# Residual rows moved to DRAM for the expert blocks, a fourth pair of weight buffers, and a transposition moved into block 14

## The chip, the core and the metric

The kernel runs on one core of a Trainium2 chip. The core has TensorE (PE), VectorE (DVE), ScalarE (ACT), GpSimd (POOL), SyncE (SP) and 16 DMA engines. The engines run their own instruction streams and wait for one another through semaphores. The metric is the time of one execution on the device, in microseconds.

## What is computed

A layer on 512 tokens of width 1024: RMSNorm, a mixer (state-space heads beside gated recurrent heads) with a residual addition, then a second RMSNorm and a mixture of 16 experts in four groups. Each token takes its best group and two experts in it. All of it is in float32.

```python
# in the layer
x = x + jnp.concatenate([y_ssd, y_hgrn], axis=-1) @ w_out[l]
h = rmsnorm(x, norm_ffn_w[l])
x = x + hier_moe(h, router_group[l], router_expert[l], w_gate[l], w_up[l], w_down[l])
...
# in hier_moe, for each expert
hid = jax.nn.silu(t @ wg) * (t @ wu)
return acc + c[:, None].astype(t.dtype) * (hid @ wd), None
...
return rmsnorm(x, final_norm_w)
```

## The kernel before

**Stages.** The front (to about 296 us) computes the mixer, the residual rows `xres` (512 rows of 1024 floats, 2 MB of SBUF in `arena`), and the normalised rows, which ScalarE stores to `h2_dram` in four column units (`store_rows`, L890). Routing follows: which tokens go to which expert. Then 16 expert blocks run, and at the end the two results of each token are read back, weighted, added to the residual row and normalised.

**A block** handles one expert `e`: GpSimd gathers up to 112 token rows from `h2_dram` into one of four buffers (`gather`, L645); TensorE transposes them; ScalarE and DVE make a high and a low part of everything that is multiplied (float32 as the sum of two reduced numbers, three products each). The weights are three loads of 1 MB: `a` (first half of gate and up, K rows 0 to 511), `b` (second half) and `c` (down). High parts come from ScalarE (`round_a`, `round_b`, `round_c`), the low part of `a` from GpSimd (`split_a`), those of `b` and `c` from DVE (`split_b` L1444, `split_c` L1450). TensorE does `gate_up_a`, `gate_up_b`; ScalarE the silu, DVE the product `hid` (`hidden`, L1456). TensorE transposes `hid` into bank 4, ScalarE rounds it to `hidh` (L969), DVE subtracts to `hidl` (L1467), and TensorE makes the down product in two halves of 512 columns (banks 5 and 6). ScalarE copies these out and GpSimd scatters them to `pairs_dram` (L675).

**Order.** `pe_expert(e)` is written out by hand and runs one block ahead: `gate_up_a(e+1)`, transposition of hid(e), transposition of the tokens of e+2, `gate_up_b(e+1)`, down product of e. In the last two blocks some of these drop out.

**Loads.** SP issues the weight loads in one fixed order, `a`(e), `c`(e-1), `b`(e). There are three buffers of each kind (`WSETS`). Before each load SP waits until the buffer's last user is split: `wla_ok`, `wlb_ok`, `wlc_ok`. SP issues in order, so a load whose buffer is free still waits behind an earlier one that waits. `b`(3) also waits for the first gather (`gat_in[0]`). After the last weights SP loads the early half of the result rows (`load_early`, L526), which DVE adds to `xres` (L1510, `early`), then, after the last scatter, the late half (`late`).

## Time and profile before

| | us |
|---|---|
| three runs: median (lowest to highest) | 490.27 (490.12 to 491.42) |
| the profiled execution: its time | 490.27 |
| its span, first to last instruction | 488.5 |
| TensorE busy | 445.9 (91% of the span) |
| DVE, ScalarE, GpSimd busy | 340.3, 272.2, 147.9 |
| DMA | 92.47 MB, 189 GB/s over the span |

Matmuls are pipelined, so TensorE's busy time is not its time at full rate. The mean granted clock of TensorE is 0.968 of full speed. The profiled execution's own time is that of the median, so differences worked out on its span can be added to the median. A wait shown for an engine is put down to the releaser that came last.

### The profile page before, as it was taken

The page shows a single profiled execution, that of the slowest core. Times are in us where ns is not written, and L with a number is a line of the kernel's source. Part 1 is how long each engine was busy: PE and PEld are TensorE (multiplying, and loading weights), DVE is VectorE, ACT ScalarE, POOL GpSimd, SP SyncE. Part 2 cuts the span into 40 slices and gives each one's busy share as a digit, 9 for nine tenths or more (in the row PEclk, how much of TensorE's full clock was granted, in tenths as well). Part 3 has the DMA queues.
Part 4 walks back from the last instruction along what each step waited for, and adds up shares of the span by engine and source line. Part 5 has one row for each costly group of instructions (what it writes and reads, how often), then busy time and mean ns, then how long its engine had stood idle before and what let it go on. Part 6 is the DMA issues. An engine that isn't in the chain of part 4 may idle for free.

```text
span 488.5 us, 7225 instructions
## 1 busy us (share of the span) xinstructions
PE 445.9 (91%) x2827; PEld 393.7 (81%) x2827; DVE 340.3 (70%) x517; ACT 272.2 (56%) x440; POOL 147.9 (30%) x113
## 2 busy tenths in 40 slices
PE   5999999999999899999899997799999999999800
PEld 3888888899898799999899996688888888887600
DVE  5424798754669777799856428678788788767847
ACT  6754273423553243226344326489899899979524
POOL 4700000000000000110510120567887987875210
PEclk9999999999999989999899998999999999999965
DMA  8622222231202111206086931569999999988345
GB/s 320 236 95 87 87 88 86 87 129 44 87 1 86 60 34 82 86 8 253 0 336 243 335 129 44 161 253 378 363 382 372 358 367 380 357 331 318 128 154 225
DMA packets 20626, 92.47 MB, mean 189 GB/s; under 512 B 4797, under 2 KB 7017, under 8 KB 12138
## 3 DMA queue, kind: packets, MB, share of 16 engines
q1 hardware_dynamic: 13848, 81.42, 44.3%
q0 software_dynamic: 4096, 8.41, 5.1%
q10 hardware_dynamic: 2642, 2.11, 1.4%
q8 instruction: 24, 0.39, 0.3%
q14 instruction: 16, 0.13, 0.1%
HBM read 86.69 MB, written 11.54 MB: 201 GB/s over the span
## 4 chain that ended last, share of the span: by engine, by line
PE 69%; DVE 13%; DMA 8%; ACT 7%; issue 2%; POOLq 0%; SPq 0%; DVEq 0%; ACTq 0%
PE bank L1578 40%; DMA arena<-in_w_gate_up_dram 5%; PE bank L1896 4%; PE bank L1898 4%; PE bank L1897 4%; PE bank L1884 2%; PE bank L1750 1%; PE bank L1766 1%; DMA pairs_dram<-arena 1%; DVE wl L1031 1%; DMA X<-h_dram,arena 1%; ACT wh L907 1%; PE bank L1648 1%; DVE arena L1542 1%; PE bank L1649 1%
## 5 line engine op out<-in xcount | busy, mean ns | idle before, releaser
L1578 PE MATMUL bank<-wh,acth 128*128 128x256 f32 x320 | 93.2, 291 | 3.3 <-DVE actl L1025 1.9
L1578 PE MATMUL bank<-wl,acth 128*128 128x256 f32 x320 | 91.8, 287 | 0.0
L1578 PE MATMUL bank<-wh,actl 128*128 128x256 f32 x320 | 91.7, 287 | 0.0
L1578 PEld LDWEIGHTS bank<-wh,acth 128*128 128x128 f32 x320 | 62.8, 196 | 3.7 <-issue 3.7
L665 POOL TENSOR_TENSOR wl<-raw,wh 128x1024 fp32r<-128x1024 f32 x21 | 50.6, 2432 | 47.3 <-ACT wh L902 47.3
L611 POOL TENSOR_TENSOR arena<-arena,bc 128x512 f32<-128x512 f32 x4 | 6.6, 1655 | 190.6 <-DVE arena L1106 190.6
L1578 PEld LDWEIGHTS bank<-wl,acth 128*128 128x128 f32 x320 | 62.9, 196 | 0.0
L1578 PEld LDWEIGHTS bank<-wh,actl 128*128 128x128 f32 x320 | 62.7, 196 | 0.0
L1896 PE MATMUL bank<-wh,acth 128*128 128x512 f32 x128 | 51.7, 404 | 1.4 <-DVE wl L1447 1.2
L1898 PE MATMUL bank<-wh,actl 128*128 128x512 f32 x128 | 50.1, 392 | 0.0
L1897 PE MATMUL bank<-wl,acth 128*128 128x512 f32 x128 | 49.9, 390 | 0.0
L1578 PE MATMUL bank<-acth,wh 128*128 128x512 f32 x112 | 44.1, 393 | 0.0
L1578 PE MATMUL bank<-acth,wl 128*128 128x512 f32 x112 | 43.6, 390 | 0.0
L1578 PE MATMUL bank<-actl,wh 128*128 128x512 f32 x112 | 43.6, 389 | 0.0
L721 ACT ACTIVATE wh<-raw 128x2048 fp32r<-128x2048 f32 x18 | 34.4, 1910 | 15.4 <-PE bank L1578 15.4
L1031 DVE TENSOR_TENSOR wl<-raw,wh 128x2048 fp32r<-128x2048 f32 x15 | 34.3, 2288 | 3.5 <-ACT wh L721 3.4
L1453 DVE TENSOR_TENSOR actl<-arena,acth 128x1024 fp32r<-128x1024 f32 x30 | 35.7, 1229 | 1.4 <-ACT acth L916 1.0
L1441 DVE TENSOR_TENSOR actl<-bank,acth 128x512 fp32r<-128x512 f32 x32 | 20.6, 686 | 18.2 <-ACT acth L954 18.0
L1447 DVE TENSOR_TENSOR wl<-arena,wh 128x1024 fp32r<-128x1024 f32 x20 | 27.0, 1388 | 8.2 <-ACT wh L907 8.2
L916 ACT ACTIVATE acth<-arena 128x1024 fp32r<-128x1024 f32 x30 | 30.0, 1056 | 0.0
L1896 PEld LDWEIGHTS bank<-wh,acth 128*128 128x128 f32 x128 | 24.0, 188 | 7.2 <-issue 2.1
L654 POOL DMA_INDIRECT X<-h_dram,arena x16 | 26.5, 1659 | 8.0 <-issue 6.8
(335 smaller groups left out, 1039.1 us busy)
## 6 DMA issues: line engine op xcount, KB each, us to landing
raw<-in_w_units_dram SPq DMA_DIRECT2D x18, 1024.0 KB, 4.8
raw<-in_w_gate_up_dram SPq DMA_DIRECT2D x17, 1024.0 KB, 11.1
arena<-in_w_down_dram SPq DMA_DIRECT2D x16, 1024.0 KB
arena<-in_w_gate_up_dram SPq DMA_DIRECT2D x15, 1024.0 KB, 12.5
arena<-pairs_dram SPq DMA_DIRECT2D x6, 512.0 KB, 6.5
X<-in_x_dram SPq DMA_DIRECT2D x4, 512.0 KB, 5.1
arena<-in_x_dram SPq DMA_DIRECT2D x1, 2048.0 KB, 9.9
h_dram<-X ACTq DMA_DIRECT2D x4, 512.0 KB, 4.0
```

The source lines that it names most:

```text
L654: gp.indirect_dma_start(hg[j][0:CAP, :], None, h2_dram, bass.IndirectOffsetOnAxis(ap=gix[0:CAP, PERM[e]:PERM[e] + 1], axis=0), bounds_chec ...
L665: gp.tensor_tensor(wl[:, 0, c], raw_a[b][:, c], wh[:, 0, c].bitcast(F32), ALU.subtract).then_inc(wla_ok, 1)
L721: sc.activation(wh[:, u % SPL, :], raw[:, u % RAW, :], ACT.Copy).then_inc(wh_ok, 1)
L916: sc.activation(down_high(e)[:, c], raw_c[e % WSETS][:, c], ACT.Copy).then_inc(whc_ok, 1)
L1031: ve.tensor_tensor(wl[:, u % SPL, :], raw[:, u % RAW, :], wh[:, u % SPL, :].bitcast(F32), ALU.subtract).then_inc(wl_ok, 1)
L1441: ve.tensor_tensor(gtl[b][:, c], bank[2 + h][:, :], gth[b][:, c].bitcast(F32), ALU.subtract).then_inc(gl_ok, 1)
L1447: ve.tensor_tensor(wl[:, 1, c], raw_b[e % WSETS][:, c], wh[:, 1, c].bitcast(F32), ALU.subtract).then_inc(wlb_ok, 1)
L1453: ve.tensor_tensor(down_low(e)[:, c], raw_c[e % WSETS][:, c], down_high(e)[:, c].bitcast(F32), ALU.subtract).then_inc(wlc_ok, 1)
L1578: ins = te.matmul(acc_ap, a, b, start=(j == 0), stop=(j == n - 1))
L1896: te.matmul(bank[b][:, :], ah, uh[:, k, :], start=(first and k == 0), stop=False)
L1897: te.matmul(bank[b][:, :], ah, ul[:, k, :], start=False, stop=False)
L1898: ins = te.matmul(bank[b][:, :], al_, uh[:, k, :], start=False, stop=(last and k == kh - 1))
```

## The change

The residual rows are stored to a new DRAM tensor `res_dram`, unit by unit, right behind each store of the normalised rows on ScalarE's DMA queue. The 2 MB of SBUF that they leave become a fourth buffer for `a` and one for `b` (`AB = 4`); `c` keeps three. SP loads `a`(3) and `b`(3) into them once all four residual stores have landed (`res_st`). The wait for the first gather is gone. After the last weights SP reads the residual rows back into `raw` (slots 0 and 2, `back`), before it reads the early result rows; these have one semaphore now in place of four. In block 14 TensorE transposes hid(15) between the two halves of its down product, and ScalarE and DVE write its two parts to `turn2` instead of `hidh`, `hidl`, which block 14 still reads.

```diff
@@ -261,7 +262,10 @@
         rnd = part(4)
         rounds = part(1).bitcast(I32)
 
+        raw_a += [arena[:, TT * D:TT * D + UNIT]]
+        raw_b += [arena[:, TT * D + UNIT:TT * D + 2 * UNIT]]
         early = [raw[:, 1, 0:D], raw[:, 1, D:2 * D], arena[:, 0:D], arena[:, D:2 * D]]
+        back = [raw[:, j, :].rearrange("p (t n) -> p t n", t=2) for j in (0, 2)]
         late = [arena[:, a:a + D] for a in range(8 * D, 12 * D, D)]
         assert ofs[0] <= 22528
 
@@ -271,6 +275,12 @@
 
         def down_low(e):
             return wl[:, 0, :] if e == NE - 1 else wcl
+
+        def hidden_high(e):
+            return turn2[:, 0, :] if e == NE - 1 else hidh[:, :]
+
+        def hidden_low(e):
+            return turn2[:, 1, :] if e == NE - 1 else hidl[:, :]
 
         gth = [acth[:, UNIT + b * D:UNIT + (b + 1) * D] for b in range(2)]
         gtl = [actl[:, UNIT + b * D:UNIT + (b + 1) * D] for b in range(2)]
@@ -493,48 +505,53 @@
...
             def sp_round(r, base, first_round=False):
-                for e in range(WSETS if first_round else 0, NE + 1):
-                    held = base + e - WSETS + 1 if e >= WSETS else base
+                for e in range(AB if first_round else 0, NE + 1):
+                    held = base + e - AB + 1 if e >= AB else base
                     if e < NE:
-                        if e == WSETS + 1:
+                        if e == AB + 1:
                             sp.wait_ge(gu_a, base + 2)
+                        elif e == 0:
+                            sp.wait_ge(early_ok, r * TT)
                         else:
-                            wait_a(sp, r, max(e - WSETS + 1, 0))
+                            wait_a(sp, r, max(e - AB + 1, 0))
                         load_a(e)
-                    if e - 1 >= (WSETS if first_round else 0):
+                    if e >= 1:
                         before_c = base + e - WSETS if e > WSETS else base
                         sp.wait_ge(wlc_ok, before_c * 2)
                         load_c(e - 1)
                     if e < NE:
-                        if e == 0:
-                            sp.wait_ge(early_ok, r * TT)
-                        else:
-                            sp.wait_ge(wlb_ok, held * 2)
-                        if first_round and e == WSETS:
-                            sp.wait_ge(gat_in[0], 16)
+                        sp.wait_ge(wlb_ok, held * 2)
                         load_b(e)
 
-            def load_early(rows_done, first_round=False):
+            def load_back(rows_done, first_round=False):
+                if first_round:
+                    wait_a(sp, 0, NE - 3)
+                    sp.wait_ge(wlb_ok, (NE - 3) * 2)
+                else:
+                    sp.wait_ge(sca_out[0], rows_done)
+                for j in range(2):
+                    sp.dma_start(back[j], res_dram[2 * j * P:2 * (j + 1) * P, :].rearrange("(t p) n -> p t n", p=P))\
+                        .then_inc(xres_in, 16)
                 for j in range(YB):
                     sp.wait_ge(sca_out[j], rows_done)
                 if first_round:
                     wait_a(sp, 0, NE - 2)
                     sp.wait_ge(wlb_ok, (NE - 2) * 2)
                 for tt in range(TT):
-                    sp.dma_start(early[tt], pairs_dram[tt * P:(tt + 1) * P, :]).then_inc(early_in[tt], 16)
+                    sp.dma_start(early[tt], pairs_dram[tt * P:(tt + 1) * P, :]).then_inc(early_in, 16)
 
             def sp_later(r, base):
                 sp_round(r, base)
-                load_early(r * (16 * PER_Y) + 16 * PER_Y)
+                load_back(r * (16 * PER_Y) + 16 * PER_Y)
 
             load_c(0)
             split_by(sp, n_in + 1)
@@ -548,10 +565,13 @@
             load_b(0)
             load_b(2)
             load_c(2)
+            sp.wait_ge(res_st, 16 * (n_front - n_in))
+            load_a(3)
+            load_b(3)
             sp_round(0, 0, True)
             sp.wait_ge(h2_ok, 2 * (n_front - n_in))
             sp.dma_start(bc[:, :], final_norm_w[None, :].broadcast_to([P, D])).then_inc(bc3_in, 16)
-            load_early((PER_Y - 1) * 16, True)
+            load_back((PER_Y - 1) * 16, True)
             n = later_rounds(sp, sp_later)
             for j in range(YB):
                 sp.wait_ge(sca_out[j], n * (16 * PER_Y))
@@ -891,27 +911,28 @@
                 act.wait_ge(h2_ok, unit_end[u] - n_in_groups)
                 c = slice(units[u][1], units[u][1] + UC)
                 act.dma_start(h2_dram[:, c].rearrange("(t p) n -> p t n", p=P), X[:, :, c]).then_inc(h2_st, 16)
+                act.dma_start(res_dram[:, c].rearrange("(t p) n -> p t n", p=P), xres[:, :, c]).then_inc(res_st, 16)
...
@@ -958,6 +979,10 @@
                 sc.activation(sil, bank[e % 2][:, 0:FE], ACT.Silu,
                               scale=hg[e % HGB][:, D:D + 1]).then_inc(sil_ok, 1)
 
+            def round_hidden(step, e):
+                act.wait_ge(hid_tr, step + 1)
+                sc.activation(hidden_high(e), bank[4][:, 0:FE], ACT.Copy).then_inc(hh_ok, 1)
+
             def act_expert(r, base, e, first_round):
                 step, b = base + e, e % 2
                 if 0 < e < NE - 1:
@@ -965,8 +990,8 @@
                 if e + 2 < NE:
                     act.wait_ge(gu_a, step + 2)
                     round_a(r, e + 2, (0,))
-                act.wait_ge(hid_tr, step + 1)
-                sc.activation(hidh[:, :], bank[4][:, 0:FE], ACT.Copy).then_inc(hh_ok, 1)
+                if e < NE - 1:
+                    round_hidden(step, e)
                 if e + 2 < NE:
                     round_a(r, e + 2, (1,))
                     round_tokens(step + 2, b)
@@ -976,6 +1001,8 @@
                     silu(step + 1, e + 1)
                 if e + 2 < NE:
                     round_b(r, e + 2)
+                elif e + 1 < NE:
+                    round_hidden(step + 1, e + 1)
                 act.wait_ge(dn, step * 2 + 3)
                 y_free(act, r, e, first_round)
                 sc.activation(ysb[e % YB][:, 0:512], bank[5][:, :], ACT.Copy).then_inc(y0_ok, 1)
@@ -1505,10 +1533,11 @@
                     dve_expert(r, base, e, first_round)
                 if first_round:
                     gates()
+                dve.wait_ge(xres_in, r * 32 + 48)
+                dve.wait_ge(early_in, r * (16 * TT) + 16 * TT)
                 for tt in range(TT):
-                    dve.wait_ge(early_in[tt], r * 16 + 16)
-                    ve.scalar_tensor_tensor(early[tt], early[tt], r1[:, 10, tt:tt + 1], xres[:, tt, :], ALU.mult,
-                                            ALU.add).then_inc(early_ok, 1)
+                    ve.scalar_tensor_tensor(early[tt], early[tt], r1[:, 10, tt:tt + 1], back[tt // 2][:, tt % 2, :],
+                                            ALU.mult, ALU.add).then_inc(early_ok, 1)
 
             def gates():
                 dve.wait_ge(ge_ok, 1)
@@ -1914,15 +1943,19 @@
                 pe.wait_ge(wlb_ok, step * 2 + 2)
                 gate_up(b, 1, range(4), False, True).then_inc(gu_b, 1)
 
-            def pe_expert(r, base, e):
-                step, b = base + e, e % 2
-                if e + 1 < NE:
-                    gate_up_a(r, step + 1, e + 1, 1 - b)
+            def turn_hidden(step):
                 pe.wait_ge(hid_ok, step + 2)
                 pe.wait_ge(hl_ok, step + 1)
                 for k in range(2):
                     ins = te.transpose(bank[4][:, k * P:(k + 1) * P], hid[:, k * P:(k + 1) * P], ident[:, :])
                 ins.then_inc(hid_tr, 1)
+
+            def pe_expert(r, base, e):
+                step, b = base + e, e % 2
+                if e + 1 < NE:
+                    gate_up_a(r, step + 1, e + 1, 1 - b)
+                if e < NE - 1:
+                    turn_hidden(step)
                 if e + 2 < NE:
                     turn_tokens(r, base, e + 2)
                 if e + 1 < NE:
@@ -1936,8 +1969,11 @@
                     terms = []
                     for k in range(2):
                         c, n = slice(k * P, (k + 1) * P), slice(h * 512, (h + 1) * 512)
-                        terms += [(hidh[:, c], c3h[:, k, n]), (hidh[:, c], c3l[:, k, n]), (hidl[:, c], c3h[:, k, n])]
+                        hh, hl = hidden_high(e)[:, c], hidden_low(e)[:, c]
+                        terms += [(hh, c3h[:, k, n]), (hh, c3l[:, k, n]), (hl, c3h[:, k, n])]
                     products(bank[5 + h][:, :], terms).then_inc(dn, 1)
+                    if e == NE - 2 and h == 0:
+                        turn_hidden(step + 1)
 
             def pe_round(r, base):
                 find_all(r)
```

The rest of the diff: `set_uses` gets the number of buffers, and `% WSETS` becomes `% AB` for the `a` and `b` buffers in the splits.

SP's queue around the first expert blocks. `raw` and `arena` hold the buffers; `in_w_gate_up_dram` is `a` (L496) or `b` (L499), `in_w_down_dram` is `c`. Before, from `a`(3) to `b`(4):

```order
L496 DMA raw<-in_w_gate_up_dram 128x2048 [waits wla_ok]
L499 DMA raw<-in_w_gate_up_dram 128x2048 [waits gat_in0,wlb_ok]
L496 DMA raw<-in_w_gate_up_dram 128x2048 [waits gu_a]
L502 DMA arena<-in_w_down_dram 128x2048 [waits wlc_ok]
L499 DMA arena<-in_w_gate_up_dram 128x2048 [waits wlb_ok]
```

After (L508 is `a`, L511 is `b`, L514 is `c`), from `a`(3) to `a`(5):

```order
L508 DMA arena<-in_w_gate_up_dram 128x2048 [waits res_st]
L511 DMA arena<-in_w_gate_up_dram 128x2048
L508 DMA raw<-in_w_gate_up_dram 128x2048 [waits wla_ok]
L514 DMA arena<-in_w_down_dram 128x2048 [waits wlc_ok]
L511 DMA raw<-in_w_gate_up_dram 128x2048 [waits wlb_ok]
L508 DMA raw<-in_w_gate_up_dram 128x2048 [waits gu_a]
```

`a`(3) and `b`(3) wait for the residual stores only, no load waits for the gather any more, and the wait for `gu_a` stands at `a`(5), behind `c`(3) and `b`(4), where it stood ahead of them at `a`(4).

TensorE's queue at the end of the blocks: the down product of block 14 (`acth`, `actl` hold its weights, `hidh`, `hidl` the products), the transposes (`ident`) and the down product of block 15 (weights in `wh`, `wl`). Before:

```order
L1578 MATMUL bank<-actl,hidh 128x512
L1578 MATMUL bank<-acth,hidl 128x512
L1924 MATMUL bank<-ident,arena 128x128 [waits hl_ok,hid_ok]
L1924 MATMUL bank<-ident,arena 128x128
L1578 MATMUL bank<-wh,hidh 128x512 [waits y0_ok,wlc_ok,hl_ok]
```

After, where the same two transposes stand:

```order
L1607 MATMUL bank<-actl,hidh 128x512
L1607 MATMUL bank<-acth,hidl 128x512
L1950 MATMUL bank<-ident,arena 128x128 [waits hl_ok,hid_ok]
L1950 MATMUL bank<-ident,arena 128x128
L1607 MATMUL bank<-acth,hidh 128x512 [waits y1_ok]
```

They moved from behind the second half (which waits for `y1_ok`) to ahead of it; the down product of block 15 now follows the second half directly and reads `turn2`.

## Rows read from the trace of the kernel before

**Rows 1.** The page's slices of 12.2 us: DMA engines' busy tenths.
```profile
DMA  8622222231202111206086931569999999988345
```

**Rows 2.** Waits of PE, 230 to 489: in total, times, longest us.
```profile
PE bank L1884 <- DMA X<-h_dram,arena: 2.5, 1, 2.5
...
PE bank L1855 <- DVE arena L1385: 2.0, 1, 2.0
...
PE bank L1578 <- DVE hidl L1467: 1.2, 1, 1.2
...
PE bank L1896 <- DVE wl L1447: 1.2, 2, 0.8
```

**Rows 3.** The chain that ended last: start us, us, what.
```profile
304.90 4.35 DMA X<-h_dram,arena
...
416.17 24.49 DMA arena<-in_w_gate_up_dram
...
465.65 5.16 DMA pairs_dram<-arena
```

**Rows 4.** PE in order of time: start us, us, line, form, [idle before].
```profile
430.22 0.39 PE L1896 MATMUL bank<-wh,acth 128*128 128x512 f32 x1
...
439.56 0.39 PE L1896 MATMUL bank<-wh,acth 128*128 128x512 f32 x1
...
450.26 0.39 PE L1896 MATMUL bank<-wh,acth 128*128 128x512 f32 x1
...
453.99 0.47 PE L1896 MATMUL bank<-wh,acth 128*128 128x512 f32 x1 [0.43 <-DVE wl L1447]
...
461.13 0.50 PE L1578 MATMUL bank<-wh,hidh 128*128 128x512 f32 x1 [1.20 <-DVE hidl L1467]
```

**Rows 5.** ACT in order of time, the second half `b` of expert 14.
```profile
440.68 2.01 ACT L907 ACTIVATE wh<-arena 128x1024 fp32r<-128x1024 f32 x2 [3.10 <-DMA arena<-in_w_gate_up_dram]
```

**Rows 6.** DMA issues of windows 295.5, 329, 338, 404, 322, 406.7, 444: KB, us to landing.
```profile
h_dram<-X ACTq DMA_DIRECT2D x1, 512.0 KB, 3.4
...
pairs_dram<-arena POOLq DMA_INDIRECT x1, 6.9
...
pairs_dram<-arena POOLq DMA_INDIRECT x1, 9.6
...
pairs_dram<-arena POOLq DMA_INDIRECT x1, 12.2
...
arena<-in_w_gate_up_dram SPq DMA_DIRECT2D x1, 1024.0 KB, 9.1
...
arena<-in_w_gate_up_dram SPq DMA_DIRECT2D x1, 1024.0 KB, 22.4
...
arena<-pairs_dram SPq DMA_DIRECT2D x2, 512.0 KB, 13.2
```

**Rows 7.** SP's queue in order of time: start us, us, what is issued.
```profile
284.48 0.33 SPq L496 DMA_DIRECT2D raw<-in_w_gate_up_dram  x1
...
309.33 0.33 SPq L499 DMA_DIRECT2D raw<-in_w_gate_up_dram  x1
...
321.17 0.33 SPq L496 DMA_DIRECT2D raw<-in_w_gate_up_dram  x1
...
332.18 0.46 SPq L499 DMA_DIRECT2D arena<-in_w_gate_up_dram  x1
...
336.49 0.33 SPq L496 DMA_DIRECT2D raw<-in_w_gate_up_dram  x1
```

**Rows 8.** Busy us of each engine, granted clock, DMA share, GB/s in a stretch.
```profile
300.00:304.00 4.00, 3.99 (x38) 3.93 (x39) 3.00 (x14) 2.03 (x3) 0.00 (x0) 0.58 0.00 0
```

**Rows 9.** DVE in order of time, from block 14 to the end.
```profile
456.38 2.35 DVE L1453 TENSOR_TENSOR wl<-arena,wh 128x1024 fp32r<-128x1024 f32 x2
458.64 0.47 DVE L1458 SCALAR_TENSOR_TENSOR arena<-bank,X,arena 128x256 f32<-128x256 f32 x1
...
474.29 2.58 DVE L1536 SCALAR_TENSOR_TENSOR arena<-arena,raw 128x1024 f32<-128x1024 f32 x2 [6.61 <-DMA arena<-pairs_dram]
```

More of the change, by code:

```diff
@@ L135, in trunk @@
     WSETS = 3
+    AB = 4
     HGB = 4
@@ L404, in trunk @@
         fin_ok = sem("fin_ok")
-        ra_in, rb_in, rc_in = ([sem(f"{n}{b}") for b in range(WSETS)] for n in ("ra_in", "rb_in", "rc_in"))
+        ra_in, rb_in = ([sem(f"{n}{b}") for b in range(AB)] for n in ("ra_in", "rb_in"))
+        rc_in = [sem(f"rc_in{b}") for b in range(WSETS)]
         gat_in = [sem(f"gat_in{j}") for j in range(HGB)]
         sca_out = [sem(f"sca_out{j}") for j in range(YB)]
-        early_in = [sem(f"early_in{t}") for t in range(TT)]
+        early_in = sem("early_in")
+        res_st = sem("res_st")
         late_in = [sem(f"late_in{t}") for t in range(TT)]
@@ L421, in trunk @@
         PERM = [(e % G) * EG + e // G for e in range(NE)]
-        IN_SET = [(NE - w + WSETS - 1) // WSETS for w in range(WSETS)]
         PER_Y = NE // YB
@@ L432, in later_rounds, with set_uses @@
             return n
-        def set_uses(r, e):
-            return r * IN_SET[e % WSETS] + e // WSETS + 1
+        def set_uses(r, e, sets):
+            return r * ((NE - e % sets + sets - 1) // sets) + e // sets + 1
         def y_free(eng, r, e, first_round):
@@ L495, in load_a @@
             def load_a(e):
-                sp.dma_start(raw_a[e % WSETS], w_gate_up[PERM[e], 0]).then_inc(ra_in[e % WSETS], 16)
+                sp.dma_start(raw_a[e % AB], w_gate_up[PERM[e], 0]).then_inc(ra_in[e % AB], 16)
             def load_b(e):
-                sp.dma_start(raw_b[e % WSETS], w_gate_up[PERM[e], 1]).then_inc(rb_in[e % WSETS], 16)
+                sp.dma_start(raw_b[e % AB], w_gate_up[PERM[e], 1]).then_inc(rb_in[e % AB], 16)
             def load_c(e):
@@ L658, in split_a @@
             def split_a(step, e):
-                b = e % WSETS
+                b = e % AB
                 for h in range(2):
@@ L899, in round_a @@
             def round_a(r, e, which=(0, 1)):
-                act.wait_ge(ra_in[e % WSETS], set_uses(r, e) * 16)
+                act.wait_ge(ra_in[e % AB], set_uses(r, e, AB) * 16)
                 for c in halves(which):
-                    sc.activation(wh[:, 0, c], raw_a[e % WSETS][:, c], ACT.Copy).then_inc(wha_ok, 1)
+                    sc.activation(wh[:, 0, c], raw_a[e % AB][:, c], ACT.Copy).then_inc(wha_ok, 1)
             def round_b(r, e):
-                act.wait_ge(rb_in[e % WSETS], set_uses(r, e) * 16)
+                act.wait_ge(rb_in[e % AB], set_uses(r, e, AB) * 16)
                 for c in halves((0, 1)):
-                    sc.activation(wh[:, 1, c], raw_b[e % WSETS][:, c], ACT.Copy).then_inc(whb_ok, 1)
+                    sc.activation(wh[:, 1, c], raw_b[e % AB][:, c], ACT.Copy).then_inc(whb_ok, 1)
             def round_c(r, base, e):
@@ L1466, in dve_expert @@
                 dve.wait_ge(hh_ok, step + 1)
-                ve.tensor_tensor(hidl[:, :], bank[4][:, 0:FE], hidh[:, :].bitcast(F32), ALU.subtract).then_inc(hl_ok, 1)
+                ve.tensor_tensor(hidden_low(e), bank[4][:, 0:FE], hidden_high(e).bitcast(F32),
+                                 ALU.subtract).then_inc(hl_ok, 1)
                 if e + 2 < NE:
```

5 lines of the change are left out of this document (3 added, 2 removed).

## The prediction

> **What bounds the kernel now.** I read first the row of the DMA engines' busy tenths over the 40 slices (12.2 us each) [rows 1]: 3, 1 and 5 tenths in slices 24 to 26 (281 to 317 us), then 6, eight times 9 and twice 8 (317 to 452 us), which is where the expert blocks run. Next, who waited for whom, on TensorE from 230 us on [rows 2]: in the blocks it waits in three places only: 2.5 us for the first gathered tokens, 1.2 us for the low part of weights (DVE L1447, the subtraction for a second half `b`), and 1.2 us for `hidl` in the last block. The chain that ended last [rows 3] runs through the same places: the gather of expert 0 (304.90, 4.35 us), then a `b` load that took 24.49 us, then the last scatter. TensorE sets the pace between 311 and 464 us, fed by a DMA that can only just keep up, and the start of the blocks hangs on one gather.
>
> The blocks themselves, from the first matmul of `gate_up_a` [rows 4]: 430.22 to 439.56 is 9.34 us for a block without a stall, 439.56 to 450.26 is 10.70 us. Block 15's `gate_up_b` should start 2.94 us after its `gate_up_a` (12 matmuls at 0.227 us and two transposes), so at 453.20; it starts at 453.99. The late weights thus cost 1.36 + 0.79 = 2.15, say **2.2 us**. Why they are late: ScalarE waits 3.10 us for `b` of expert 14 [rows 5]. The time from issue to landing of a `b` load grows from 9.1 us (expert 4, issued at 322.0) to 22.4 us (expert 13, issued at 406.8) [rows 6]: 13.3 us over nine blocks, 1.5 us per block. The DMA needs about 10.8 us for what a block of 9.33 us uses, and lives on its lead.
>
> **The fourth pair and the order of the loads.** Where the loads are issued now [rows 7]: `a`(3) at 284.48, `b`(3) at 309.33 (held until the first gather has landed), `a`(4) at 321.17 with `c`(3) and `b`(4) behind it, `c`(4) and `b`(5) at 332, `a`(6) at 336.49. After the change `a`(3), `b`(3) wait for the residual stores. The last h2 store takes 3.4 us from issue [rows 6]; the residual store of equal size goes behind it and adds 0.524 MB at some 340 GB/s, 1.5 us: issued at 296.0, landed at about 301. `a`(3), `b`(3) and `a`(4) then go out in a row at 301 to 302 and `c`(3), `b`(4) at about 310.5, when DVE has split `c`(0). `a`(5) waits for `gu_a`, 321.2. From there SP's order decides: `c`(4) still needs the three-deep `c` buffers (the split of `c`(1), 331.8), and `b`(5) stands behind it in SP's queue, so `b`(5) goes out at 332.2 **as before**, and only `a`(6) is early, by 4 us, in a queue that is full anyway. The fourth pair does not give a block's lead; it gives a queue that is emptier at 332 us.
> How much emptier: before, six loads were issued from 321.2 to 332.2. By row `b`(4), three loads and the latency take 9.9 us (321.17 to 331.1), and later loads 3.6 us each (10.8 by three), so `b`(5) lands at some 341.5. After, `c`(4) and `b`(5) meet an empty queue: two loads, 7.2 us less what the emptiness saves, landing at 338 to 340. The lead gained is 1.5 to 3.6 us, I take 2.6. `b`(14) was 3.1 us late at ScalarE and becomes 0.5 late; 1.06 us of lateness one block earlier cost TensorE nothing, the block of `a`(15) starting on its 9.34 us. Both late subtractions are then in time: **−2.2 us** (bounds −1.0, if the lead is 1.5 and the gain half, and −2.2, since no more is lost there). What is next: TensorE itself at 9.33 us per block.
>
> **The price at the start.** Between 300 and 304 us the DMA share is 0.00 today, and the gather of expert 0 has the engines to itself: 4.35 us from 304.90 [rows 3, 8]. After, it enters at about 306.2, behind three weight loads of 1 MB (8.5 us of transfers from 303 on). No row shows a gather under load with its landing. The nearest are scatters of equal size on the same queue [rows 6]: 6.9 us (329, three or four loads outstanding), 9.6 us (338), 12.2 us (404, a deep backlog), against 5.16 us alone (465.65) [rows 3]. So load costs +1.7, +4.4 or +7.0 us. At 306 three loads are outstanding, as at 329 and 338: between +1.7 and +4.4, **+3.3 us** taken. Lower bound 0.5 (the gather is a read and reaches few rows), upper +7, which would also take in expert 1's gather: it is issued 1.5 us after the first and is needed 4.9 us after it. All of it is on the path: TensorE, ScalarE (high part) and DVE (low part) wait for this landing in turn.
> The trace shows full DMA share with the scatter still through in 6.9 us, far less than the backlog of the weight queue. The Trainium skill (DMA: Bandwidth & Descriptors, Queues, rings and completion order) says that each DMA engine takes turns between its queues, a packet at a time. By that rule a gather shares instead of queueing, about doubling its moving part of 2 to 3 us: the sum would be nearer +2 than +3.3, and both stay inside the bounds.
>
> **The residual rows.** Added: four stores of 0.5 MB on ScalarE's queue, two reads of 1 MB, four times 0.4 us of ScalarE for issuing. The first three stores fall before 281 us, where the loads in flight are wanted no sooner than 296; ScalarE has 0.8 us of idle time after each. The store of `rs` moves behind the last residual store, from 299.3 to about 301; the gather itself waits for the index table until 303.5. Cost 0, cover 2.5 us; past it each us counts. SP waits at `res_st` instead of loading `a`(3) at 284.48: wanted at 330, cost 0. At the end the reads (5.6 us of DMA time) stand between `c`(15) and the early rows, which landed 13.2 us after issue at 444.43 [rows 6], at 457.6: with the reads at about 463, less the lead. DVE's additions of the early rows end 6.61 us before 474.29, at 467.7, and then it waits for the late rows [rows 9]; they take 5 us, so they begin at 462.8. Cost 0 while the reads delay them by less than 6.6 us, beyond that fully. DVE, waiting there, has nothing else queued but the final sums.
>
> **Block 14.** Today the last transposes follow the down product of block 14; ScalarE and DVE then make hidh and hidl, and the down product of block 15 starts at 461.13 after a wait of 1.20 us [rows 4], 1.36 us after the transposes end. Now the transposes go between its two halves of 1.38 us. But hid(15) must exist: DVE L1458 ends at 459.11, behind the split of `c`(15) (456.38, 2.35 us) [rows 9], whereas the first half ends at 458.18. On this trace TensorE would wait 1.0 us in the middle and gain only 0.35. With `b`(15) in time the same order gives more: `gate_up_a` of block 15 starts at D, the first half ends at D+7.1, hid is ready at D+7.5 by these durations, the second half ends at D+9.2, and block 15's down product starts there instead of at D+10.0. **−0.8 us** (bounds −0.3 and −1.4, the whole wait).
>
> **Sum** against the profiled execution (span 488.5, time 490.27, which is also the median): +3.3 − 2.2 − 0.8 = +0.3, so a span of 488.8 and **490.6 us**. The tail after the last matmul, 24 us, stays.
>
> **Rivals.**
> (1) The gather is hardly disturbed (up to +1.5). Then 490.27 + 1.0 − 3.0 = **488.3**, faster. For: only three loads are outstanding and the shallowest scatter lost 1.7. Against: 9.6 us at 338 with the same number.
> (2) The start slips by 5 us or more: gather 0 at +4.4 to +7 and gather 1 behind it in the same queue late as well, or TensorE's clock falls. It was granted 0.58 from 300 to 304 [rows 8], the lower level of 1.2 GHz for most of it, after a wait of 2.0 us for the routing [rows 2]; after the 2.5 us at 306.8 it stayed high. With the idle time at 5 us or more a second fall may follow, costing some 1.7 us of doubled matmuls. 490.27 + 5.5 − 3.0 = **492.8**, up to 495. It decides once the gather takes more than 8.7 us.
> (3) The lead does nothing at the end: the queue fills again at 1.5 us per block and `b`(14), `b`(15) are as late, since SP's order issues them when it did. Then +3.3 − 0.3 (block 14 on late weights) gives **493.3**. Against: a later start of TensorE gives the DMA that much more time before each need, so part of the lateness goes in any case.
> (4) The change doesn't do what it says: `b`(e) is not issued earlier from expert 5 on. That is already in the sum.
>
> **How the numbers follow.** Forecast case (+1.5 to +4.5 at the start, stalls gone): 0.45, own range 488.9 to 491.8. Rival 1: 0.27. Rival 2: 0.18. Rival 3: 0.10. The range 487.3 to 494.3 leaves out the ends of rivals 1 and 2. A measurement can tell 0.3% (1.5 us) from no change: faster means under 488.8, slower over 491.7. Rival 1 nearly all faster, with a little of the forecast case: 0.30. Rivals 2 and 3 and the upper end of the forecast case: 0.32. Same: 0.38.
>
> **What would show it.** Gather of expert 0 from issue to landing 7 to 8 us instead of 4.35, TensorE's first wait 5 to 6 us instead of 2.5. `a`(3) issued at 301, `b`(5) within 0.5 us of `c`(4). No wait of ScalarE for a `b` load above 2 us and no TensorE wait for DVE L1447's successor. A short TensorE wait between the halves of block 14, none before block 15's down product. DVE's early additions no later than 468 relative to the same end. Wrong if the gather lands in 5 us, if `b` loads late in the run still take over 22 us, or if the late rows are waited for longer than 6.6 us.

## The result and the profile after

| | before | after |
|---|---|---|
| median of one job, us | 489.21 (20 runs) | 492.6 (20 runs) |
| span of the profiled execution | 488.5 | 492.1 |
| DMA | 92.47 MB, 189 GB/s | 96.67 MB, 196 GB/s |

The ratio is 1.0071, 95% interval 1.0049 to 1.0092: the change costs 3.5 us (2.4 to 4.5). I had said 490.6 on 490.27 for the likeliest case, inside 0.3% of no change; the time lies in the range of the prediction, but above that case. By the 0.3% that I had set as the border it is slower, to which I had given 0.32 (no change 0.38).

The page's slices of 12.3 us of the kernel after, the DMA engines' busy tenths; they answer to [rows 1]:

```profile
DMA  8622223240202213033189908727999999989455
```

Slices 25 and 26 (295 to 320 us), which hold the gather, have 8 and 7 tenths where there were 1 and 5; slices 27 and 28 have 2 and 7 where [rows 1] has 6 and 9. The loads moved forward, and behind them a hole opened.

TensorE's waits after, from 230 us on (in total, times, longest), as in [rows 2]; L1925 is the second half of gate and up, L1950 the transposition of `hid`:

```profile
PE bank L1913 <- DMA X<-h_dram,arena: 5.8, 1, 5.8
PE bank L1884 <- DVE arena L1412: 2.0, 1, 2.0
...
PE bank L1925 <- DVE wl L1474: 1.0, 2, 0.6
PE bank L1950 <- DVE arena L1485: 0.8, 1, 0.8
```

The wait for the gathered tokens grew from 2.5 to 5.8 us; that for the low part of `b` is still there; the 1.2 us for `hidl` became 0.8 us between the halves of block 14. The chain that ended last (start us, us, what) runs through the same three transfers as in [rows 3]:

```profile
302.86 7.79 DMA X<-h_dram,arena
...
419.65 24.70 DMA arena<-in_w_gate_up_dram
...
469.02 5.35 DMA pairs_dram<-arena
```

The gather takes 7.79 us instead of 4.35, the `b`(14) load 24.70 instead of 24.49, the last scatter 5.35 instead of 5.16.

TensorE in order of time, after:

```profile
310.69 1.97 PE L1913 MATMUL bank<-ident,X 128*128 128x128 f32 x8 [5.84 <-DMA X<-h_dram,arena]
312.45 1.91 PE L1589 MATMUL bank<-upto,ones 128*128 128x128 f32 x8
314.01 0.77 PE L1925 MATMUL bank<-wh,acth 128*128 128x512 f32 x1
...
462.89 0.44 PE L1950 MATMUL bank<-ident,arena 128*128 128x128 f32 x2 [0.80 <-DVE arena L1485]
463.08 0.48 PE L1607 MATMUL bank<-acth,hidh 128*128 128x512 f32 x1
...
464.56 0.40 PE L1607 MATMUL bank<-wh,turn 128*128 128x512 f32 x1
```

The eight transposes after the gather take 1.97 us; at the end of a gather that came in 4.2 us (version e1, below) the same eight take 1.09. So TensorE comes back at half its clock. The windows say the same (stretch; its length; busy time of PE, its weight loads, DVE, ScalarE and GpSimd, each with a count; granted clock; DMA share; GB/s):

```profile
305.00:307.00 2.00, 0.00 (x0) 0.00 (x0) 2.00 (x3) 0.00 (x0) 1.70 (x2) 1.00 1.02 426
307.00:309.00 2.00, 0.00 (x0) 0.00 (x0) 1.49 (x2) 0.00 (x0) 1.70 (x2) 1.00 0.77 239
309.00:311.00 2.00, 0.31 (x2) 0.32 (x3) 0.00 (x0) 0.00 (x0) 0.50 (x1) 0.53 0.81 257
311.00:313.00 2.00, 2.00 (x11) 2.00 (x10) 0.53 (x1) 0.91 (x2) 0.00 (x0) 0.50 1.03 287
313.00:315.00 2.00, 2.00 (x9) 1.82 (x8) 0.85 (x2) 0.29 (x1) 0.00 (x0) 0.50 1.01 353
```

TensorE idles from 304.85 to 310.69; the clock falls from 2.4 to 1.2 GHz at about 309, before the tokens are there, and stays there until after 315.

**Where the 3.6 us of span come from.** Each execution can be cut at the same four points of TensorE's queue. G is the time from the issue of the first gather to the first transposes of its tokens, C from there to the transposes of expert 1's tokens, then come twelve blocks, and E is the time from the transposes of expert 13's tokens to the last matmul. The twelve blocks take 109.56 to 109.60 us in all fourteen profiles of this study; so all that differs is in G, C, E, in the front (to the gather's issue) and in the tail (last matmul to the end).

| | front | G | C | E | tail |
|---|---|---|---|---|---|
| before | 304.90 | 4.39 | 4.95 | 40.34 | 24.33 |
| after | 302.86 | 7.83 | 7.05 | 40.21 | 24.57 |
| difference | −2.04 | +3.44 | +2.10 | −0.13 | +0.24 |

The sum is +3.6 us. The front's −2.04 can't be put down to the change: the front ends between 301.6 and 304.9 in the fourteen executions, at 303.2 on average in the four without the residual stores and at 303.7 in the ten with them. The tails lie between 23.7 and 25.8. The gather gives +3.44, the lower clock +2.10, and the end, where I had taken off 3.0 us, gives back 0.1.

### The profile page after: what moved, and what is told of

Its sections match the earlier page's. It is cut to its first block, busy times and chain, and to the rows that moved or that the text cites. A ratio compares the mean times of both kernels' runs of the same rounds, so it can differ in the third digit from the quotient of the medians.

```text
span 492.1 us, 7231 instructions
## 1 busy us (share of the span) xinstructions
PE 446.3 (91%) x2827; PEld 393.5 (80%) x2827; DVE 340.3 (69%) x517; ACT 272.3 (55%) x440; POOL 147.2 (30%) x113
## 2 busy tenths in 40 slices
DMA packets 23282, 96.67 MB, mean 196 GB/s; under 512 B 4893, under 2 KB 9161, under 8 KB 14794
## 4 chain that ended last, share of the span: by engine, by line
PE 68%; DVE 14%; DMA 9%; ACT 7%; issue 2%; POOLq 0%; SPq 0%; DVEq 0%; ACTq 0%
PE bank L1607 39%; DMA arena<-in_w_gate_up_dram 5%; PE bank L1925 4%; PE bank L1927 4%; PE bank L1926 4%; PE bank L1913 2%; DMA X<-h_dram,arena 2%; DMA pairs_dram<-arena 1%; PE bank L1779 1%; PE bank L1795 1%; DVE actl L1480 1%; DVE wl L1058 1%; ACT wh L928 1%; PE bank L1589 1%; PE bank L1677 1%
## 5 line engine op out<-in xcount | busy, mean ns | idle before, releaser
L1925 PE MATMUL bank<-wh,acth 128*128 128x512 f32 x128 | 52.3, 409 | 1.1 <-DVE wl L1474 1.0
L685 POOL TENSOR_TENSOR wl<-raw,wh 128x1024 fp32r<-128x1024 f32 x15 | 36.0, 2419 | 50.1 <-ACT wh L923 50.1
L685 POOL TENSOR_TENSOR wl<-arena,wh 128x1024 fp32r<-128x1024 f32 x16 | 39.0, 2457 | 13.0 <-ACT wh L923 13.0
L1474 DVE TENSOR_TENSOR wl<-arena,wh 128x1024 fp32r<-128x1024 f32 x24 | 33.6, 1438 | 9.0 <-ACT wh L928 8.9
L1925 PEld LDWEIGHTS bank<-wh,acth 128*128 128x128 f32 x128 | 24.3, 190 | 7.1 <-issue 1.9
```

Of the source, the lines that this page charges most:

```text
L685: gp.tensor_tensor(wl[:, 0, c], raw_a[b][:, c], wh[:, 0, c].bitcast(F32), ALU.subtract).then_inc(wla_ok, 1)
L1474: ve.tensor_tensor(wl[:, 1, c], raw_b[e % AB][:, c], wh[:, 1, c].bitcast(F32), ALU.subtract).then_inc(wlb_ok, 1)
L1925: te.matmul(bank[b][:, :], ah, uh[:, k, :], start=(first and k == 0), stop=False)
```

## Experiments

Ratios are to the kernel before in the same job, with their 95% interval. All profiles are cut at the points named above. In a clean end, with no weight late, E is 37.01 us with the move in block 14 (e2, f2, g1) and 38.12 without it (g2); "late" is E less that.

**e1: the gather alone again.** The kernel after, with `a`(3) and `b`(3) held until the first gather has landed:

```diff
             sp.wait_ge(res_st, 16 * (n_front - n_in))
+            sp.wait_ge(gat_in[0], 16)
             load_a(3)
             load_b(3)
```

> The changed kernel, but SP also waits for the first gather before it loads a(3), b(3), a(4). My theory: the disturbed gather (7.79 us in place of 4.35) and the slow matmuls behind it (2.1 us) are the whole loss. Then the gather lands in 4.3 to 4.6 us, transposes of expert 1 follow the first gather by 5.0 us in place of 7.05, and the time falls 5 us below the changed kernel, to 1 to 2 us below the kernel before if the block 14 edit gives 0.3 and the late weights stay as they are. Rival: the loss is the extra 4 MB of traffic or the later a(3); then the time stays within 1 us of the changed kernel (3.4 us over before).

Measured: ratio 1.0006 (0.9979 to 1.0032). G 4.20, C 4.94, E 39.18, so late 2.17. The loss is gone, so it sat at the start. No gain is left over, though there are four pairs of halves.

What the gather meets: DMA packets of the kernel after in the first 4 us from the gather's issue (q1 is SP's queue, q0 the one of the gather):

```profile
DMA packets 224, 1.70 MB, mean 426 GB/s; under 512 B 16, under 2 KB 16, under 8 KB 16
## 3 DMA queue, kind: packets, MB, share of 16 engines
q1 hardware_dynamic: 223, 1.70, 100.6%
```

and in the rest, up to its landing at 310.65:

```profile
q0 software_dynamic: 337, 0.58, 52.5%
q1 hardware_dynamic: 58, 0.34, 23.9%
```

In e1, in the same first 4 us and, in the second fence, without the first 1.5 of them (304.67 to 308.67, and 306.17 to 308.67):

```profile
q0 software_dynamic: 176, 0.25, 26.6%
```

```profile
q0 software_dynamic: 176, 0.25, 42.5%
```

The count is the same, so none moves in the first 1.5 us; in e1 and in the kernel before the first packet comes 1.8 to 1.9 us after the issue. Under three weight loads not one of them moves in the first 4 us, while q1 fills all 16 engines; its first packet comes 4.4 to 4.5 us after the issue, as the loads run out. The five executions with these three loads ahead of the gather (after, e3, f2, f3, f4) show what the start follows: counted from the gather's own issue the first packet comes after 3.5 to 4.5 us, counted from the issue of `a`(3) after 8.8 to 9.1 us in all five. So the gather does not share with the loads, it begins behind them, and then takes some 3.3 us (7.79 less 4.45) for what takes 2.5 alone (4.35 less 1.85). The Trainium skill (DMA: Bandwidth & Descriptors, Queues, rings and completion order) says that an engine goes round the queues that have work, packet by packet; what the trace shows between 304.4 and 306.9 is no such turn-taking, and both queues are at work only after that. Whether this goes against the page stays open: if the gather's descriptors came late, its queue had no work to take turns with; if they were there, its packets were passed over. No run here tells the two apart.

**e3 and f3: is it the clock?** The kernel after, with more dummy matmuls while TensorE waits for the gather; nothing reads their result. e3 has 36 more, f3 has 24 more:

```diff
                 find_targets(r)
-                keep_warm(4)
+                keep_warm(4 + 36)
                 turn_tokens(r, base, 0)
```

> The changed kernel with 36 more dummy matmuls of 128 columns ahead of the first token transposes, so that TensorE is busy for 5 of the 5.8 us in which it waits for the gather. Theory: the slow transposes and the slow first matmuls (0.63 to 0.77 us each) come from the longer idle time. Then the transposes take 1.1 us as before, the expert 1 transposes follow by 5.0 us in place of 7.05, and the time is 2 us below the changed kernel. Rival: the slow start is something else, such as reads of tokens under DMA load; then nothing changes, within 0.5 us.

> As e3_warm with 24 repetitions in place of 36: there the dummies ran on for about 2 us after the gather had landed, and with them the matmuls behind ran at full clock. Theory: with 24 they end within 0.5 us of the landing, the slow matmuls stay away, and the time from the gather's issue to the end of the last down product is 162.3 to 163 us in place of 164.7 of the changed kernel; 1.5 to 2.3 us under the changed kernel by the clock. Rival: within 0.5 us of the changed kernel.

Measured: e3 1.0100 (1.0066 to 1.0134), f3 1.0041 (1.0019 to 1.0063); the kernel after, again beside f3 in one job, 1.0088 (1.0053 to 1.0123). In e3 the dummies run until 314.2, past the landing: G is 9.92 and C 4.87. They cost 2.1 us of G and give 2.2 of C, and the time is no better than that of the kernel after. In f3 they end as the tokens come, TensorE in order of time:

```profile
305.64 6.50 PE L1589 MATMUL bank<-upto,ones 128*128 128x128 f32 x56
312.29 0.98 PE L1913 MATMUL bank<-ident,X 128*128 128x128 f32 x7 [0.15 <-DMA X<-h_dram,arena]
```

G is 7.58, as in the kernel after, and C is 4.93 in place of 7.05. Full clock, same gather: f3 is 2.3 us faster than the kernel after by the ratios, where the two C differ by 2.1. The intervals overlap, so the time alone would not prove it; profile and time together say that the clock costs about 2 us.

**f4: the change again**, as it is.

> The changed kernel again, beside the others on the same chip. Theory: 3.4 us over before (1 to 5.5), the gather lands 7.5 to 8 us after its issue and slow matmuls follow it. Rival: the clock fell only in the one profiled execution; then the gather is as slow here but the tokens of expert 1 are turned 4.9 to 5.1 us after those of expert 0.

Its profile has G 7.75 and C 7.09, as in the first one. But E is 38.08: late 1.07 instead of 3.20. The late weights differ by 2 us between two executions of one kernel, so one profile can't price them; this bears on every E here.

**e2: the order of the loads.** e1, and `b`(e) asked for ahead of `c`(e-1):

```diff
                         load_a(e)
+                    if e < NE:
+                        sp.wait_ge(wlb_ok, held * 2)
+                        load_b(e)
                     if e >= 1:
                         before_c = base + e - WSETS if e > WSETS else base
                         sp.wait_ge(wlc_ok, before_c * 2)
                         load_c(e - 1)
-                    if e < NE:
-                        sp.wait_ge(wlb_ok, held * 2)
-                        load_b(e)
```

> As e1_hold, and SP issues a(e), b(e), c(e-1) in place of a(e), c(e-1), b(e), so that b(e) no longer stands behind the wait for a c buffer. My theory: the fourth pair gave nothing in the blocks because of that order. Then b(5) is issued about one block (9 us) earlier, ScalarE no longer waits for b(13) and b(14), block 13 to 15 run at 9.33 us and the time is 1.5 to 2.5 us below e1_hold. Rival: the DMA is behind by its rate alone (about 10.8 us of transfers for each block of 9.33 us), whatever the order; then landing times of b change but the ScalarE waits of 2 us stay within 0.5 us and the time is that of e1_hold.

Measured: 486.62 us, ratio 0.9954 (0.9926 to 0.9982). G 4.53, C 4.92, E 37.02: no load is waited for any more. SP's queue, `b`(14) in e1 and, in the second fence, in e2:

```profile
415.73 0.43 SPq L511 DMA_DIRECT2D arena<-in_w_gate_up_dram  x1
```

```profile
407.25 0.42 SPq L511 DMA_DIRECT2D arena<-in_w_gate_up_dram  x1
```

8.5 us earlier, nearly one block, which is what a fourth buffer should give. And the stretch in which that lead can be made, in the kernel after, in e1 and in e2, one fence each (columns as above, DMA share next to last):

```profile
317.00:324.00 7.00, 6.90 (x35) 5.47 (x35) 4.33 (x6) 5.35 (x7) 2.41 (x1) 1.00 0.14 58
324.00:330.00 6.00, 6.00 (x33) 5.05 (x32) 3.60 (x6) 4.70 (x8) 4.21 (x2) 1.00 0.48 175
330.00:340.00 10.00, 10.00 (x51) 8.35 (x50) 8.03 (x9) 9.16 (x13) 8.17 (x5) 1.00 0.51 172
```

```profile
324.00:330.00 6.00, 6.00 (x28) 4.91 (x27) 5.12 (x6) 5.24 (x7) 5.44 (x4) 1.00 0.85 348
330.00:340.00 10.00, 10.00 (x54) 8.47 (x53) 8.07 (x10) 9.05 (x13) 7.56 (x4) 1.00 0.91 347
```

```profile
317.00:324.00 7.00, 6.90 (x36) 5.51 (x35) 5.26 (x7) 5.64 (x9) 2.71 (x2) 1.00 1.01 379
324.00:330.00 6.00, 6.00 (x28) 4.87 (x27) 5.12 (x6) 5.30 (x8) 5.54 (x4) 1.00 0.97 403
330.00:340.00 10.00, 10.00 (x54) 8.47 (x53) 8.07 (x10) 8.96 (x13) 7.56 (x4) 1.00 0.91 343
```

In the kernel after, the DMA engines are half idle from 324 to 340 us: 16 us at some 0.5, 8 us of transfers not made, though `b`(5) had its buffer (before that, from 317 to 324, they have 0.14, as in the kernel before 0.28, since `a`(5) waits for `gu_a` until 324.64): e2 asks for it 7.7 us after the transposes of expert 1's tokens, the kernel after 17.9 us after them. SP's queue shows why, from `a`(3) on, after:

```profile
298.24 0.33 SPq L508 DMA_DIRECT2D arena<-in_w_gate_up_dram  x1
...
308.52 0.33 SPq L514 DMA_DIRECT2D arena<-in_w_down_dram  x1
...
324.64 0.33 SPq L508 DMA_DIRECT2D raw<-in_w_gate_up_dram  x1
335.27 0.33 SPq L514 DMA_DIRECT2D arena<-in_w_down_dram  x1
335.64 0.55 SPq L511 DMA_DIRECT2D arena<-in_w_gate_up_dram  x1
```

`c`(4) waits for its buffer until 335.27, and `b`(5) goes out right behind it. `a`(5) went out at 324.64, and nothing between.

But the idle stretch is not what makes the weights late at the end. e1 has the same order and starts its loads 10 us later; its engines stand at 0.85 and 0.91 from 324 to 340 us, and it is late by 2.17 all the same. e1 and e2 differ only in the order, and with it goes the time at which each `b` is asked for.

**f2 and f1: the order without the hold, and the order alone.** f2 is the kernel after with the new order and no hold; f1 is the kernel before with `b`(e) ahead of `c`(e-1), three pairs.

> The changed kernel with the order a(e), b(e), c(e-1) but without the wait for the first gather. My theory: hold and order are separate. The gather takes 7.5 to 9 us (four loads ahead of it in place of three), the clock falls behind it, and the late weights vanish: 2 to 3 us under the changed kernel, 0.5 to 2 us over before. Rival: with the order mended the early loads are worth their price; then it is as fast as e2_hold_order, 2.5 us under before.

> The kernel before with one edit: SP issues a(e), b(e), c(e-1) in place of a(e), c(e-1), b(e). It tells whether the fourth pair is needed for what the order gave in e2_hold_order (2.5 us below before). Theory A: the order alone does it, since b(e) is held by the wait for the c buffer and not by its own. b(5) then goes out 2 to 3 us earlier relative to the tokens of expert 1, ScalarE's waits for b(13), b(14) shrink from 4.2 us to under 2 us, and the time is 1 to 2 us under before. Theory B: without the fourth pair b(e) can be issued only 2.8 us earlier and c gets behind; then the time is within 1 us of before.

Measured: f2 1.0062 (1.0034 to 1.009), G 7.37, C 7.45, late 0. f1 0.998 (0.9951 to 1.001), G 4.32, C 7.40, late 1.24. The order mends the end of f2 and leaves it the start. And it does so with DMA engines that are far from full at the beginning of the blocks, which f2 reaches 1 us sooner than the kernel after:

```profile
323.00:329.00 6.00, 6.00 (x33) 5.04 (x33) 3.61 (x6) 4.67 (x8) 4.14 (x2) 1.00 0.69 254
329.00:339.00 10.00, 10.00 (x51) 8.36 (x49) 8.08 (x9) 9.16 (x14) 8.24 (x5) 1.00 0.67 229
```
 In f1, with three pairs, other loads are late; who ScalarE waited for there, from 400 us on:

```profile
ACT wh L902 <- DMA arena<-in_w_gate_up_dram: 1.2, 1, 1.2
ACT acth L916 <- DMA arena<-in_w_down_dram: 1.0, 2, 0.9
ACT wh L902 <- DMA raw<-in_w_gate_up_dram: 0.6, 1, 0.6
```

L902 is `a`, L916 is `c`: the lateness went over from `b` to them.

**e4: block 14 alone.** The kernel before with the transposes of hid(15) between the halves of block 14 and the products in `turn2`, nothing else of the change.

> The kernel before with only the block 14 part of the change. On the trace of before the transposes wait about 1.0 us for the product of expert 15, since DVE splits the last down weights first. Theory: gain 0.3 to 0.5 us, a TensorE wait of 0.8 to 1.0 us between the halves of block 14, none before the last down product. Rival: the whole wait of 1.2 us goes, gain 1.2 to 1.4 us.

Measured: 0.9994 (0.9968 to 1.002). TensorE's waits:

```profile
PE bank L1909 <- DVE wl L1459: 1.5, 2, 1.0
PE bank L1934 <- DVE arena L1470: 0.8, 1, 0.8
```

The 1.2 us wait of [rows 4] became one of 0.8 us between the halves, as the `hid` product isn't ready. From the transposes of expert 15's tokens to the last matmul e4 takes 21.61 us, the kernel before 21.67.

**g1, g2, g3: what the best version is made of.** One job. g1 is e2 again. g2 is g1 with block 14 as in the kernel before. g3 is f1 with the move in block 14, so that it lacks only the fourth pair and the residual rows in DRAM.

> The version with the hold on the gather and with the down matrix asked for after the two halves, once more, beside two neighbours on one chip. Computes all that the reference asks for. Theory (the change loses at the gather by competition and by the clock, and the halves come late only since c(e-1) stands ahead of b(e)): ratio to the kernel before 0.995, between 0.992 and 0.998. A rival (the first result was a lucky one): 0.999 to 1.001.

> The version g1 with the block-14 part undone: the silu products of the last block are turned after block 14, as in the kernel before; residual rows in DRAM, four pairs of halves, the hold and the order stay. Theory A (the move is worth what its wait leaves over: block 14 and 15 together shrink by 0.4 to 0.8 us, since the weights are no longer late there): 0.4 to 0.8 us slower than g1. Rival B (with the weights on time the products wait for the activation in either place, and the move is worth nothing): within 0.2 us of g1.

> The kernel before with the new order of the loads (a, b, then c of the expert before) and with the block-14 part; three pairs of halves, residual rows in on-chip memory, nothing in DRAM. Theory A (the fourth pair is what keeps the halves on time once the order is right: here some b is still late, by 0.5 to 1 us in all, as in the run with the order alone): 0.5 to 1.5 us slower than g1. Rival B (the order alone does it, the fourth pair and the residual rows in DRAM are worth nothing): within 0.4 us of g1, ratio to the kernel before 0.995.

| | us | ratio (95%) | G | C | E | late |
|---|---|---|---|---|---|---|
| g1 | 486.37 | 0.9938 (0.9911 to 0.9964) | 4.45 | 7.29 | 37.01 | 0 |
| g2 | 486.84 | 0.9963 (0.9934 to 0.9992) | 4.32 | 7.39 | 38.12 | 0 |
| g3 | 488.12 | 0.9984 (0.9951 to 1.0018) | 4.34 | 4.95 | 39.03 | 2.02 |

g1 is faster than both kernels, as e2 was. With the weights on time the move in block 14 is worth 1.11 us in the profile (38.12 less 37.01); the medians differ by 0.5, and their intervals overlap. g2's last block waits as the kernel before did:

```profile
PE bank L1605 <- DVE hidl L1492: 1.2, 1, 1.2
```

g3 has late weights, 2.02 us. All four profiles with four pairs and the new order have none (e2, f2, g1 and g2); the two with the new order and three pairs have 1.24 and 2.02; the five with four pairs and the old order have 1.07 to 3.23. It takes both. By time, g1 to g3 is 1.8 us with overlapping intervals.

**h1: the residual stores alone.** The kernel before with the four stores, which nobody reads; the only wait on them stands ahead of the early rows:

```diff
                 act.dma_start(h2_dram[:, c].rearrange("(t p) n -> p t n", p=P), X[:, :, c]).then_inc(h2_st, 16)
+                act.dma_start(res_dram[:, c].rearrange("(t p) n -> p t n", p=P), xres[:, :, c]).then_inc(xres_in, 16)
```

> The kernel before with the four stores of the residual rows to DRAM on ScalarE's queue and nothing else of the change: nobody reads them back, three pairs of buffers, the old order. The stages measured on single profiles add up to times that are some 1 us too short for the kernels with the residual rows in DRAM; the front, whose end moves by 3 us from one execution to the next, could hide that much. Theory A (the stores cost nothing, as predicted): within 0.5 us of the kernel before, ratio 0.999 to 1.001. Rival B (0.4 us of ScalarE for each of the four issues, and 2 MB more on the queue before the last normalised rows land, delay the front): 0.5 to 2 us slower, ratio 1.001 to 1.004. In both the gather takes 4.3 to 4.7 us, with no weight load beside it.

Measured: 1.0009 (0.998 to 1.0038). The interval, −1 to +1.9 us, holds both theories, so this isn't settled. The profile has G 4.44, C 4.94, late 2.58, and its front ends at 304.11, among the others.

## Why the prediction was right or wrong, point by point

**The time: in the range, but not by the forecast case.** Two things that I had kept apart as rivals came together: the clock fell (rival 2, 492.8 alone) and the weights stayed late (rival 3, 493.3 alone). By my own figures the two together give 490.27 + 3.3 + 1.7 − 0.3 = 495.0, above the range of 487.3 to 494.3. That the time stayed inside is in part luck.

**What bounds the kernel: right.** Twelve blocks take 109.6 us in each of the fourteen profiles, whatever the loads do.

**The gather, +3.3: right in size, wrong in kind.** It measured +3.44, and +3.36 in f4. I had leaned on scatters under load. The gather neither shares, by which I had worked out +2, nor queues by halves: its packets don't start until the weight loads are nearly through. So the +3.4 is mostly the remainder of three loads asked for 4.6 us before the gather.

**The clock, rival 2: this is the step that failed.** Rival 2 says that a second fall may come with an idle time of 5 us or more, and then that it decides once the gather takes more than 8.7 us. The two don't fit. By [rows 2] the wait is 2.5 us with a gather of 4.35; with +3.3 it is 5.8, which is the forecast case itself. The fall belonged into the forecast's sum, with the 1.7 us that I had priced it at (measured: 2.10 in the profiles). With it the likeliest time would have been 492.3.

**The late weights, −2.2: failed.** Late by 2.22 us before; 3.20 and 1.07 in two executions of the kernel after, 2.12 to 3.23 in e1, e3 and f3. Over these five profiles the mean is 2.4, that of the three with three pairs and the old order (before, e4, h1) 2.7. So −0.3 in place of −2.2, and that is less than executions differ among themselves. The `b`(14) load took 24.70 us, over the 22 that I had named as a sign of being wrong. The step was the lead: I had seen that `b`(5) goes out no earlier, and still took 2.6 us of lead from a queue that is emptier at 332 us. The emptier queue did come, half of the 16 us before 340 were not used, and it was worth nothing at the end; e1, with a nearly full one, is as late. What `b`(14) lacked was an earlier issue: in e2 it is asked for 8.5 us sooner than in e1, and nothing is late. ScalarE's waits for `b` at the end, after, beside 3.10 us in [rows 5]:

```profile
433.62 2.01 ACT L928 ACTIVATE wh<-arena 128x1024 fp32r<-128x1024 f32 x2 [1.98 <-DMA arena<-in_w_gate_up_dram]
...
444.38 2.01 ACT L928 ACTIVATE wh<-arena 128x1024 fp32r<-128x1024 f32 x2 [2.38 <-DMA arena<-in_w_gate_up_dram]
```

The prediction named this as rival 3, at 0.10, and put against it that a later start of TensorE gives the DMA more time. But SP's waits hang on the same blocks: when they start later, so do the loads.

**Block 14, −0.8: right, under its condition.** 1.11 us with the weights on time (bounds 0.3 to 1.4), and 0.06 with late ones (e4), where I had worked out 0.35. Since the weights stayed late, the kernel after had less of it: a wait of 0.80 us stands between the halves.

**The residual rows, 0: not refuted.** At the end it holds: DVE's early additions start at 468.81 after a wait of 2.98 us, and then it still waits 4.22 us for the late rows, against 6.61 in [rows 9]. DVE in order of time, after:

```profile
468.81 2.48 DVE L1539 SCALAR_TENSOR_TENSOR raw<-raw,arena 128x1024 f32<-128x1024 f32 x2 [2.98 <-DMA arena<-pairs_dram]
...
477.91 2.48 DVE L1565 SCALAR_TENSOR_TENSOR arena<-arena,raw 128x1024 f32<-128x1024 f32 x2 [4.22 <-DMA arena<-pairs_dram]
```

So the read-back eats 2.4 us of a slack of 6.6, and the tails differ by 0.24 us. At the front h1 leaves between −1 and +1.9 us.

**The sum as measured:** gather +3.4, clock +1.3, late weights −0.3, block 14 −1.1: +3.3, where the time says +3.5 (2.4 to 4.5). The clock counts 1.3 and not 2.1, because it also falls in three of the nine profiles with a short gather, at 2.4 us each (below): 2.1 less a third of 2.4. The split of the last two terms is loose, since e4, one of the three that give 2.7, has the move in block 14 and is late by 3.26. Without a split, E is 40.5 on average in the two with neither part (before, h1) and 39.4 in the five (after, e1, e3, f3, f4): −1.2 for both, where I had taken −3.0, and a sum of +3.5. What stays open: the first bookkeeping gives e1 −1.4 us, and its interval ends at −1.0; it gives f2 +0.9 (gather 3.0, clock 2.5 less 0.8, late weights −2.7, block 14 −1.1), and its interval begins at +1.7. By the second these are −1.2 and +1.2, and both are still below their intervals. Some tenths of a microsecond to one, in the kernels with the residual rows in DRAM, are not accounted for. The front ends 0.5 us later in them on average, but its spread of 3.3 us makes that no evidence, and h1 could not tell.

## What to carry to other kernels

A further buffer gives lead only to a load that can be issued: in a queue that is worked off in order, look at what each load stands behind, and compare the time at which it is issued with the time at which its buffer comes free. How full the DMA engines are in between tells little: e1 at 0.85 to 0.91 was late and f2 at 0.67 to 0.69 was not. A transfer moved forward should be checked against the small, latency-bound one that it now overtakes; here one wait on one semaphore was worth more than the buffer. When an idle time of TensorE grows, put the clock into the sum by the wait that the sum itself gives, not by a threshold of its own.

## What the hardware showed that I had not expected

**A gather behind weight loads does not start until they are nearly through.** G is 4.20 to 4.53 us in eight of the nine profiles in which nothing runs beside the gather, and 4.70 in the other, and 7.37 to 7.83 in the four with three 1 MB loads outstanding and TensorE not held by dummies (after, f2, f3, f4).

**The clock falls in short waits too, in some executions.** With a wait of 5.8 or 5.9 us it fell each time (after, f2, f4). With 0.5 to 3.0 us it fell in three of nine: f1, g1 and g2. Granted clock in 2 us stretches, g3 and, in the second fence, g1:

```profile
306.00:308.00 2.00, 0.63 (x6) 0.44 (x4) 2.00 (x3) 0.00 (x0) 1.70 (x2) 1.00 0.39 107
308.00:310.00 2.00, 1.31 (x12) 1.31 (x13) 1.93 (x2) 0.62 (x2) 1.70 (x2) 1.00 0.67 156
```

```profile
306.00:308.00 2.00, 0.00 (x0) 0.00 (x0) 2.00 (x2) 0.00 (x0) 1.70 (x2) 0.75 0.45 109
308.00:310.00 2.00, 1.92 (x9) 1.92 (x10) 1.40 (x3) 0.60 (x1) 1.70 (x2) 0.50 0.63 185
```

In g3 and five others the clock had been at its lower level between 298 and 309 us, in the routing or just behind it, and stood high again when the blocks began; in f1, g1 and g2 it had been low earlier, from about 292 to 300, was high from 302 to 304, and fell again in the wait for the gather. C is then 7.29 to 7.40 us instead of 4.92 to 4.95. These three also have the longest waits of the nine: 2.9, 3.0 and 2.9 us, against 0.5 to 2.5 us in the six that stayed high. The two go together: where the clock is high in the routing, TensorE is through sooner and waits longer (it reaches the wait 1.4 us after the gather's issue in g1, 1.9 in the kernel before, 2.2 in g3). So these executions don't tell whether the length of the wait or the time since the last low stretch decides. For the wait speak after and f4: they were low from 299 to 302 us, as e4 was, which waited 2.2 us and stayed high. f2, with its long wait, has the history of f1. So even with a start like that of the kernel before, a fall that costs 2.4 us came in three of nine. That part of the spread of its times comes from this is likely, but no run here showed it. The Trainium skill (TensorE: Matmul & The Clock Gate, Part 1) says that the activity is watched in a free-running window, so that one kernel can meet it in different phases; the two histories in the traces fit that, and none tests it.
